# Interleaving the hi and lo parts of the standing operands, and shifting where they begin

## Time and profile before

| | |
|---|---|
| median of the two runs | 1163.97 us |
| the profiled execution | 1163.91 us |
| its span (first to last instruction) | 1162.2 us |
| granted TensorE clock, mean | 0.998 |
| PE busy | 1153.9 us (99%), 5573 matmuls |
| PEld (weight loads) busy | 945.9 us (81%) |
| DVE busy | 951.5 us (82%) |
| ACT busy | 581.7 us (50%) |
| read from memory | 209.28 MB, 181 GB/s |

### The profile page before, as it was taken

One profiled execution on the slowest core, in us unless ns is written; L12 is line 12 of the kernel. 1 busy time (PEld: TensorE's weight loads), 2 busy tenths in 40 slices (PEclk: granted clock), 3 DMA queues, 4 the chain that ended last, 5 costly groups with the idle time before them and its releaser, 6 DMA issues.

```text
span 1162.2 us, 16328 instructions
## 1 busy us (share of the span) xinstructions
PE 1153.9 (99%) x5573; PEld 945.9 (81%) x5573; DVE 951.5 (82%) x1788; ACT 581.7 (50%) x757; POOL 31.9 (3%) x67
## 2 busy tenths in 40 slices
PE   9999999999999999999999999999999999999997
PEld 7888888887778888888888888888877788888886
DVE  6877788899977687778887887878999696888777
ACT  6444345447764464344454444454578635434433
POOL 2000000001000000000000000000010000000000
PEclk9999999999999999999999999999999999999999
DMA  8566554765425555655556556556653335655561
GB/s 285 190 214 216 181 188 163 234 203 163 137 80 182 181 157 204 217 191 185 195 177 202 180 173 215 182 189 191 198 180 110 141 135 184 219 181 169 202 234 38
DMA packets 148996, 211.04 MB, mean 182 GB/s; under 512 B 8160, under 2 KB 109136, under 8 KB 148944
## 3 DMA queue, kind: packets, MB, share of 16 engines
q1 hardware_dynamic: 148256, 209.64, 54.5%
q10 hardware_dynamic: 688, 0.71, 0.2%
HBM read 209.28 MB, written 1.05 MB: 181 GB/s over the span
## 4 chain that ended last, share of the span: by engine, by line
PE 99%; DVE 0%; issue 0%; ACT 0%; POOLq 0%; POOL 0%; DVEq 0%
PE ps L1371 30%; PE ps L1373 30%; PE ps L1372 30%; PE ps L1585 2%; PE ps L1421 1%; PE ps L1641 1%; PE ps L1613 1%; PE ps L1390 1%; PE ps L1546 1%; PE ps L1558 0%; PE ps L1765 0%; PE ps L1672 0%; PE ps L1632 0%; DVE x L1000 0%; PE ps L1573 0%
## 5 line engine op out<-in xcount | busy, mean ns | idle before, releaser
L1114 ACT ACTIVATE whi<-raw 128x2048 fp32r<-128x2048 f32 (+1 forms) x195 | 365.9, 1879 | 253.3 <-PE ps L1373 252.2
L536 DVE TENSOR_TENSOR wlo<-raw,whi 128x2048 fp32r<-128x2048 f32 (+1 forms) x195 | 433.9, 2244 | 65.6 <-ACT whi L1114 45.7
L1371 PE MATMUL ps<-whi,ht_hi 128*128 128x512 f32 (+1 forms) x1192 | 465.6, 391 | 0.2
L1373 PE MATMUL ps<-whi,ht_lo 128*128 128x512 f32 (+1 forms) x1192 | 460.8, 387 | 0.0
L1372 PE MATMUL ps<-wlo,ht_hi 128*128 128x512 f32 (+1 forms) x1192 | 460.3, 386 | 0.0
L1373 PEld LDWEIGHTS ps<-whi,ht_lo 128*128 128x128 f32 x1192 | 223.9, 188 | 45.9
L1371 PEld LDWEIGHTS ps<-whi,ht_hi 128*128 128x128 f32 x1192 | 224.0, 188 | 45.0 <-issue 1.4
L1372 PEld LDWEIGHTS ps<-wlo,ht_hi 128*128 128x128 f32 x1192 | 224.1, 188 | 43.9
L598 DVE STREAM_TRANSPOSE scr<-scr 32x128 f32<-32x128 f32 x688 | 208.3, 303 | 10.3
L1371 PE MATMUL ps<-whi,at_hi 128*128 128x512 f32 x304 | 118.5, 390 | 0.0
L1372 PE MATMUL ps<-wlo,at_hi 128*128 128x512 f32 x304 | 118.3, 389 | 0.0
(11 more groups left out here) (176 smaller groups left out, 757.3 us busy)
## 6 DMA issues: line engine op xcount, KB each, us to landing
raw<-in_ffn_w_down_dram SPq DMA_DIRECT2D x88, 512.0 KB, 4.9
raw<-in_w_in_dram SPq DMA_DIRECT2D x88, 512.0 KB, 4.5
raw<-in_ffn_w_gate_dram SPq DMA_DIRECT2D x85, 512.0 KB, 4.0
raw<-in_ffn_w_up_dram SPq DMA_DIRECT2D x85, 512.0 KB, 5.0
raw<-in_w_out_dram SPq DMA_DIRECT2D x16, 512.0 KB, 4.4
raw<-in_w_branch_c_dram SPq DMA_DIRECT2D x8, 512.0 KB, 4.4
raw<-in_w_branch_b_dram SPq DMA_DIRECT2D x4, 512.0 KB, 3.9
raw<-in_w_branch_a_dram SPq DMA_DIRECT2D x4, 512.0 KB, 4.0
```

What stands on the lines that cost most here:

```text
L536: nc.vector.tensor_tensor(wlo[:, n, 0:w], raw[:, n, 0:w], whi[:, n, 0:w].bitcast(F32), ALU.subtract).then_inc(lo_done, 1)
L1114: nc.scalar.activation(whi[:, n, 0:w], raw[:, n, 0:w], ACT.Copy).then_inc(hi_done, 1)
L1371: nc.tensor.matmul(o, xh, wh, start=start, stop=False)
L1373: return nc.tensor.matmul(o, xl, wh, start=False, stop=stop)
```

## The change

The six standing tensors become three, `ht`, `at`, `bt`, with hi and lo next to each other: element 0 of a pair is hi, element 1 is lo. The names `ht_hi`, `ht_lo` and so on are now views with a step of two elements, and every use of them reads or writes with that step; no instruction is added, removed or moved, on any engine or queue. A load of 128 standing columns then reads 128 values that lie 8 bytes apart, over 1024 bytes. Four small tensors (`nmax` of 128 bytes a row, `cgt` of 192, `den` of 128, `top8` of 64) are moved in front of and between them, so `ht`, `at` and `bt` begin 128, 64 and 192 bytes on from the moving operands modulo 256. The four together have 512 bytes, so what follows keeps its place modulo 256.

```diff
-        ht_hi = sb("ht_hi", [P, KD, SEQ], F32R)
-        ht_lo = sb("ht_lo", [P, KD, SEQ], F32R)
-        at_hi = sb("at_hi", [P, 2, SEQ], F32R)
-        at_lo = sb("at_lo", [P, 2, SEQ], F32R)
-        bt_hi = sb("bt_hi", [P, 2, SEQ], F32R)
-        bt_lo = sb("bt_lo", [P, 2, SEQ], F32R)
+        nmax = sb("nmax", [P, 2, 16])
+        ht = sb("ht", [P, KD, SEQ, 2], F32R)
+        ht_hi, ht_lo = (ht[:, :, :, e] for e in range(2))
+        cgt = sb("cgt", [P, NT, 24])
+        at = sb("at", [P, 2, SEQ, 2], F32R)
+        at_hi, at_lo = (at[:, :, :, e] for e in range(2))
+        den = sb("den", [P, 2, 16])
+        bt = sb("bt", [P, 2, SEQ, 2], F32R)
+        bt_hi, bt_lo = (bt[:, :, :, e] for e in range(2))
+        top8 = sb("top8", [P, NT, 8])
         scr = sb("scr", [P, 4 * SEQ])
...
-        top8 = sb("top8", [P, NT, 8])
...
-        nmax = sb("nmax", [P, 2, 16])
-        den = sb("den", [P, 2, 16])
         rden = sb("rden", [P, 2, 16])
-        cgt = sb("cgt", [P, NT, 24])
```

## The result

The changed kernel takes 1183.67 us (two runs, 1183.31 and 1184.04) against 1163.97 us before: the ratio is 1.0169, with a 95% interval of 1.0126 to 1.0213. It is slower by 19.7 us. That lies in the stated range (1150 to 1205 us), and the ratio lies within 2%, though its interval reaches just past it. It is not the 1164 us that was forecast as likeliest: the kernel did change, and in the place and by the price that the prediction had given to a rival with a chance of 0.20. The range holds the result only because it was stretched upwards for that rival; the reasoning behind the forecast did not come true.

A forecast was written before the change was run, and what follows sets the result against it. The prediction took TensorE's pace, 4608 matmuls at 226.7 ns, to bound the kernel. Stepped loads, offsets and stepped writes added 0 + 0 + 0 to the profiled 1163.91 us, giving 1164 us, with a range of 1150 to 1205 us.

The forecast's parts named there:

- What bounds the kernel: TensorE's pace: 4608 matmuls of 512 columns at 226.7 ns, 90% of the span; each nanosecond is worth 4.6 us.
- Step 1: 4608 + 96 loads with a step of two: taken as costing nothing; bounds -4.6 us and +16 us.
- Step 2: Where ht, at and bt begin: other offsets worth between -1 and +0 ns; taken as nothing.
- the change can neither win nor lose anything in the pace: TensorE's pace: drawn from the skill's rule of two independent read ports, for the moving operand and for loads.
- The natural experiment: Matmuls before attention's small products, no load under them: 388 ns against 389 with one, so the load costs about 1 ns.
- The second clock: ScalarE's start after such a matmul: 0.43 us without a load under it, 0.42 with one, so no saved 13 ns.
- Step 3: VectorE's and ScalarE's stepped writes of hi and lo: taken as nothing; at most twice as long, 2 us exposed at the start.
- the stepped load disturbs the moving stream: Rival, chance 0.20, at all 4608 matmuls: 4 ns gives 1182 us; 10 ns gives 1210 us, taken as its time.
- the 13.3 ns: Excess of the 226.7 ns pace over 213.3 ns at full clock; about 1 ns given to the load, the rest to streaming.

The follow-up runs named there:

- experiment 1: Against the changed kernel: the small tensors go back, so the stepped ht, at and bt all begin at offset 0; 1193.74 us, ratio 1.0256.
- experiment 2: Against the kernel before: six separate unstepped tensors, small ones in between, so the pairs begin at offsets 128, 64 and 192; 1188.05 us, ratio 1.0208.
- experiment 10: Against the kernel before: only the lo tensors moved off offset 0 (ht_lo 128, at_lo 192, bt_lo 128), hi ones at 0; 1182.61 us in one run.
- 3: Against the kernel before: the second of each three wide and tall matmuls loads 32 of 128 standing columns and writes 32 rows; 1181.5 us in one run.
- 8: Against the kernel before: every wide or tall product that neither begins nor ends an accumulation loads 32 of 128 standing columns; 1181.88 us in one run.
- experiment 11: Against the kernel before: wlo alone begins 128 bytes later, standing operands untouched; 1182.52 us in one run.

## Why the prediction was right, and where it was wrong

That the measured time lies in the range is in part luck: both steps on which the 1164 us rest, loads and offsets that cost nothing, failed, and the rival that held the size had half of the mechanism.

**What bounds the kernel** was right: nearly all of the result is a change of TensorE's pace, 4608 matmuls times 4.2 ns = 19.3 us. The sensitivity (4.6 us a nanosecond) did the rest.

**Step 1, stepped loads, costed at nothing on the pace with a lower end of -1 ns.** The load's own time was right: 194 to 196 ns for 188, far from doubled, and hidden. The price on the pace failed: alone, the step cost 30 us (experiment 1). The bounds that I gave this step (a dearer load, or none) did not hold the thing that happened; only the rival did.

**Step 2, the offsets, "between -1 and +0 ns".** This is the step that failed outright. Alone, the offsets cost 24 us (experiment 2). The reasoning was: the load costs the stream about 1 ns now, so it cannot cost much elsewhere. But "now" was the one arrangement of all that I tried in which the two run in step: offset 0 modulo 256, unstepped, 128 columns. Six offsets with a step of two, five without one (32 to 192), a shifted `wlo` and narrow loads all gave mean paces of 229 to 234 ns, with single kinds of matmul below that (227.9 ns for L1374 in experiment 10). The interference measured in the one even arrangement says nothing about its neighbours. The prediction's sentence that the change can neither win nor lose anything in the pace is answered by the same numbers: the two reads do meet, and the measurement decides.

**The natural experiment** was read too far. In the earlier trace rows a matmul without a load under it ends as late as one with. There are sixteen such matmuls in front of attention's small products. Before, fourteen of them lasted 388 ns and two 397; in the changed kernel fourteen last 396 to 398 ns, 9 more, still with no load under them. The second clock agrees in nanoseconds, though not in the two decimals of a timeline: ScalarE started 426 ns after such a matmul's start before, and 434 or 435 ns after it now. (The 0.43 and 0.42 us that the prediction compared were both 426 ns.) Here is one:

```profile
285.82 0.40 PE L1373 MATMUL ps<-whi,ht 128*128 128x512 f32 x1
...
286.15 0.41 PEld L1585 LDWEIGHTS ps<-k_t,q_t 64*128 64x128 f32 x5 [0.36 <-issue]
...
286.25 0.69 ACT L1220 ACTIVATE gates<-ps,hrstd 128x512 f32<-128x512 f32 x1 [0.85 <-PE ps L1373]
```

As I read it, the time from a matmul's recorded start to its end carries delay that it inherits, so it cannot isolate what a load costs. What I drew from it, that little was to be won, was not refuted: no mean pace of the eleven experiments lies below 226.6 ns, and loading a quarter of the columns won nothing (3 and 8).

**Step 3, the writers,** was right: VectorE unchanged, ScalarE 3 to 8% longer per operation, PE still 99% busy. A load slower in itself showed only at the matmuls of 220 columns, 0.6 us in all against the 10.6 us that were the bound.

**The rival "the stepped load disturbs the moving stream"** named the place (every wide matmul) and at its mild end the size (4 ns, 1182 us; measured 4.2 ns, 1183.67). Its mechanism was half of it: what disturbs is not that the load asks for bytes faster, but where load and stream stand to each other; the step only changes that relation too. Its remark that the offsets might keep the two apart is borne out in part: with the step, offsets of 64 and 96 give 230.2 to 230.5 ns, offset 0 gives 233.7.

**What stays open.** Why offset 0 modulo 256 is the fast case, and what the 13.3 ns over 512 columns at 2.4 GHz are made of: no run streams several matmuls with no load under any, which would show whether the load costs anything even there. The repeating sequences (3 to 9 matmuls long) and experiments 10 and 11 fit the reading that one matmul's end sets how the next load and stream meet; what they meet in was not measured, nor why experiment 1 has two beats. A standing operand interleaved in runs of four values would separate lines from step; it wasn't tried.

No version was faster than the kernel before; the best of the others, all shifted together, is equal to it.

## What to carry to other kernels

Where TensorE is the bound and each matmul hides the next load, read the start-to-start distance in nanoseconds, and check whether it is even. In these runs the stretches with a repeating pattern of unequal distances were slower than the even 226 to 227 ns; but an even beat is no proof of the best one, since experiment 1 had one at 233 to 234 ns. Treat the byte offset between standing and moving operands modulo 256 as a tuning parameter that any new small tensor can disturb; here moving one tensor, `wlo`, by 128 bytes cost 1.6%. And don't infer from a small present interference that other layouts are free; the nearest row may be the exception.

## What the runs showed of the hardware that I had not expected

| step of the load | offset modulo 256 | distance, ns | load, ns |
|---|---|---|---|
| 1 | 0 (also all shifted, and 256) | 226.6 to 227.4 | 188 |
| 1 | 32, 64, 96, 128, 192 | 233.2, 233.3, 233.8, 232.4, 229.2 | 188 |
| 2 | 0, 32, 64, 96 | 233.7 (experiment 1, mean of two beats), 232.3, 230.3, 230.2 | 193 to 196 |
| 2 | 128, 192 | 231.5, 233.3 | 195 |
| 4 | 64, `at` and `bt` together | 237.9 | 310 |
| 1, mostly 32 columns | 0 | 231.2 | 109 |

With narrower loads and products the matmuls came further apart, not closer; shifting all operands together by 128 bytes did not matter, shifting one against the other did; and a matmul got slower though neither its own stream nor the load under it had moved (experiment 11).
